# First stage with more landing places and a quarter-wise first B projection, and the modulation columns added at an earlier point of each group

## What is computed

```python
def modulation(cvec, w, b):                       # ada_w: 2048 x 12288
    return split(silu(cvec) @ w + b, 6, axis=-1)  # for c and for c_ctx

mx, mc = modulation(c, ada_w, ada_b), modulation(c_ctx, ada_w, ada_b)
hx = modulate(rms_norm(x, norm_g[0]), mx[0], mx[1])      # shift, scale
hc = modulate(rms_norm(ctx, norm_g[0]), mc[0], mc[1])
# mixer: z, x, B, C, dt = split(h @ w_in)  (w_in: 2048 x 10368), depthwise convolution of
# 3 taps and silu on x, B, C; dt = softplus(dt + bias); the scan over chunks, both directions;
# y * silu(z), norm, @ w_out
x = x + mx[2] * yx
h = modulate(rms_norm(x, norm_g[1]), mx[3], mx[4])
x = x + mx[5] * hier_moe(h)        # top-1 of 4 groups, top-2 of 8 experts
```

## Time and profile before

| | us |
|---|---|
| median of 3 runs (2378.75 to 2379.55) | 2378.75 |
| the profiled execution, its own time | 2375.91 |
| its span in the trace | 2374.4 |
| until the first product of the B projection | 152.3 |
| until the first product of the first x projection | 178.0 |
| one group in the hardware loop | 119.7 |
| expert loop, from its first weights in use | 1418.3 |

### The profile page before, as it was taken

One profiled execution on the slowest core, in us unless ns is written; L12 is line 12 of the kernel. 1 busy time (PEld: TensorE's weight loads), 2 busy tenths in 40 slices (PEclk: granted clock), 3 DMA queues, 4 the chain that ended last, 5 costly groups with the idle time before them and its releaser, 6 DMA issues. The chain is left out here.

```text
span 2374.4 us, 28701 instructions
## 1 busy us (share of the span) xinstructions
PE 2048.1 (86%) x10596; PEld 1224.0 (52%) x10596; DVE 1014.8 (43%) x1625; ACT 487.0 (21%) x513; POOL 108.4 (5%) x148
## 2 busy tenths in 40 slices
PE   4679989898989898986699669888888888888887
PEld 2248767676767777774588453333333333333332
DVE  2254555555656464644554552222222222222223
ACT  3133333333333333332344310000000000000000
POOL 0000000000000000000650000000000000000000
PEclk8689999999999999998899769999999999999999
DMA  6977556565656565654555519999999999999997
GB/s 220 323 228 242 174 175 182 178 181 176 181 176 181 175 182 175 186 174 163 181 195 195 195 58 404 422 422 422 422 422 422 422 422 422 422 422 422 422 422 318
DMA packets 296347, 660.37 MB, mean 278 GB/s; under 512 B 15936, under 2 KB 186304, under 8 KB 241904
## 3 DMA queue, kind: packets, MB, share of 16 engines
q1 hardware_dynamic: 288672, 635.27, 72.2%
q0 software_dynamic: 6672, 24.29, 2.7%
q10 hardware_dynamic: 960, 0.23, 0.0%
HBM read 653.28 MB, written 6.46 MB: 278 GB/s over the span
## 5 line engine op out<-in xcount | busy, mean ns | idle before, releaser
L1590 PE MATMUL bank<-wt,xe 128*64 128x512 f32 x2048 | 466.1, 597 | 110.8 <-DMA wt<-in_moe_w_up 107.4
L1371 PE MATMUL bank<-hTh,whi 128*128 128x256 f32 (+1 forms) x1280 | 417.2, 346 | 0.0
L1372 PE MATMUL bank<-hTl,whi 128*128 128x256 f32 (+1 forms) x1280 | 408.2, 339 | 0.0
L1263 DVE TENSOR_TENSOR x<-x,bank 128x512 f32<-128x512 f32 x256 | 158.5, 682 | 543.4 <-PE bank L1577 543.4
L1590 PEld LDWEIGHTS bank<-wt,xe 128*64 128x64 f32 x2048 | 158.2, 137 | 412.9 <-issue 409.2
L1371 PEld LDWEIGHTS bank<-hTh,whi 128*128 128x128 f32 x1280 | 246.1, 192 | 86.4 <-issue 62.0
L1372 PEld LDWEIGHTS bank<-hTl,whi 128*128 128x128 f32 x1280 | 246.1, 192 | 24.1
L866 DVE TENSOR_TENSOR wlo<-raw,whi 128x2048 fp32r<-128x2048 f32 x81 | 185.5, 2291 | 138.7 <-ACT whi L642 135.0
L1376 PE MATMUL bank<-hTh,wlo 128*128 128x256 f32 (+1 forms) x1280 | 234.9, 336 | 0.0
L1615 PE MATMUL bank<-wt,hdn 128*64 128x512 f32 x1024 | 226.8, 595 | 1.4 <-DVE hdn L1275 1.4
L1376 PEld LDWEIGHTS bank<-hTh,wlo 128*128 128x128 f32 x1280 | 199.8, 190 | 24.9
(11 more groups left out here) (281 smaller groups left out, 1821.9 us busy)
## 6 DMA issues: line engine op xcount, KB each, us to landing
wt<-in_moe_w_gate SPq DMA_DIRECT2D x128, 1024.0 KB, 23.4
wt<-in_moe_w_up SPq DMA_DIRECT2D x128, 1024.0 KB, 25.5
wt<-in_moe_w_down SPq DMA_DIRECT2D x128, 1024.0 KB, 22.4
raw<-in_ada_w SPq DMA_DIRECT2D x96, 1024.0 KB, 5.2
raw<-in_ssm_w_in SPq DMA_DIRECT2D x81, 1024.0 KB, 6.1
raw<-in_ssm_w_out SPq DMA_DIRECT2D x32, 1024.0 KB, 4.8
bc<-cum_d POOLq DMA_DIRECT2D x32, 512.0 KB, 7.0
y_d<-ybuf POOLq DMA_DIRECT2D x32, 128.0 KB, 4.5
```

Of the source, the lines that this page charges most:

```text
L1263: dve.tensor_tensor(x1[:, tt, cols], x1[:, tt, cols], banks[(1, 3, 6, 7)[nb]][:, :], ALU.add).then_inc(s_acc2, 1)
L1371: pe.matmul(bank[:, 0:width], wh[:, k, :], hTh[:, k, 0:width], start=(k == 0), stop=False)
L1372: last = pe.matmul(bank[:, 0:width], wh[:, k, :], hTl[:, k, 0:width], start=False, stop=False)
L1590: last = pe.matmul(banks[0][SLOTS * h:SLOTS * h + SLOTS, :], xe[:, k, :], wt[2 * q + h][:, FF * i:FF * i + FF], start=(k == 0), stop=(k == ...
```

## The change

It has two parts.

**First stage.** Six more places of 8 KB a partition (`fr0` to `fr5`) are laid over halves of tensors that are not yet written or no longer read: the upper halves of `hTh` and `hTl` and the second half of `xrows`. A table `FSLOT` gives each of the 33 positions one of nine places. The rows of `x` and `ctx` are issued ahead of all tiles. Blocks 0 and 1 both come before the transposes; blocks 2 to 5 follow, then half of the dt projection with half of the B projection (`b_part`), then blocks 6 and 7 and the other halves. The tile of the B weights is fetched right after the dt tile. ACT and DVE share the row scaling and the copies of `xnT`. The last three small parameter loads get a semaphore of their own, so TensorE's first transposes don't wait for them. The first B convolution stands inside the dt chain, and `dt_turn` with its copies comes after the first x projection, in other banks.

**Groups.** In step 5, DVE adds the modulation columns ahead of `store` and `weights(s, 1)`.

```diff
-    PRE = ADA1 + 1
+    FRONT = ADA1 + 1
+    FSLOT = [0, 1, 2, 3, 4, 5, 6] * 2 + [7, 8, 3, 4, 5, 6, 7, 8, 3, 4, 5, 6, 7, 8, 4, 6, 7, 8, 4]
+    PRE = RAW * FSLOT.count(0)
+        fr = [at(f"fr{i}", kb, [P, D]) for i, kb in enumerate((16, 24, 48, 56, 136, 144))]
...
@@ SyncE
-            for pos in range(PRE):
-                if pos == RAW:
-                    sp.dma_start(xrows[:, 0:2, :], ...x...).then_inc(s_x, 16)
-                    sp.dma_start(xrows[:, 2:4, :], ...ctx...).then_inc(s_x, 16)
-                if pos >= RAW:
-                    front_free(pos - RAW)
+            sp.dma_start(xrows[:, 0:2, :], ...x...).then_inc(s_x[0], 16)
+            sp.dma_start(xrows[:, 2:4, :], ...ctx...).then_inc(s_x[1], 16)
+            for pos in range(FRONT):
+                before = [q for q in range(pos) if FSLOT[q] == FSLOT[pos]]
+                if before:
+                    front_free(before[-1])
+                elif FSLOT[pos] >= 7:
+                    sp.wait_ge(s_xt, KC)
                 front_load(pos)
+                if pos == DT_POS:
+                    front_free(max(q for q in range(FRONT) if FSLOT[q] == 0))
+                    sp.dma_start(w_view(raw, 0), w_in[:, :, bass.ds(w_in_at(0, 0), P)]).then_inc(s_raw[0], 16)
...
@@ ScalarE
-            for tt in range(4):
+            for tt in (0, 2):
                 act.activation(xrows[:, tt, :], xrows[:, tt, :], ACT.Copy, scale=rstd[:, tt:tt + 1]).then_inc(s_xn, 1)
+            for k in range(1, KC, 2):
+                act.wait_ge(s_xt, k + 1)
+                act.activation(xnT[:, k, :], banks[k % 2][:, :], ACT.Copy).then_inc(s_xteA, 1)
...
             round_rows(0)
-            act.wait_ge(s_raw[DT_POS % RAW], 16 * (DT_POS // RAW + 1))
-            act.activation(whi[:, 0, :], raw[:, DT_POS % RAW, :], ACT.Copy).then_inc(s_hi, 1)
-            for j in range(1, len(BLOCK_PAIRS)):
+            round_rows(1)
+            act.wait_ge(front_sem(DT_POS), 16 * (FNTH[DT_POS] + 1))
+            act.activation(whi[:, 0, :], front_tile(DT_POS), ACT.Copy).then_inc(s_hi, 1)
+            conv_hi(0, 0)
+            for j in range(2, len(BLOCK_PAIRS)):
                 round_rows(j)
-            conv_hi(0, 0)
             conv_hi(0, 1)
...
+            conv_first(0, 0)
             act.wait_ge(s_du, 1)
             act.activation(dtw[:, 3, :], dtw[:, 2, :], ACT.Ln).then_inc(s_dln, 1)
...
@@ VectorE
             ada_rows(0)
-            for k in range(KC):
+            ada_rows(1)
+            for k in range(0, KC, 2):
                 dve.wait_ge(s_xt, k + 1)
-                dve.tensor_copy(xnT[:, k, :], banks[k % 2][:, :]).then_inc(s_xte, 1)
-            ada_rows(1)
+                dve.tensor_copy(xnT[:, k, :], banks[k % 2][:, :]).then_inc(s_xteV, 1)
             modulated(0)
...
             ada_rows(2)
             ada_rows(3)
-            lo(0, 0, raw[:, DT_POS % RAW, :], free=False)
             modulated(1)
+            lo(0, 0, front_tile(DT_POS), free=False)
+            conv_lo(0, 0)
...
             dve.tensor_scalar(dtw[:, U, :], dtw[:, E, :], 1.0, None, ALU.add).then_inc(s_du, 1)
+            drain(0, 0)
             dve.wait_ge(s_du, 1)
...
@@ VectorE, steps(g, w, ssd)
                     if w and n + 1 == NCH and not (isinstance(g, int) and g == GROUPS - 1):
                         conv_lo(g + 1, 0)
+                    if w and n == 5:
+                        ada_columns(g, 0)
...
                     if w and n == 8:
                         masked(g)
-                    if w and n == 5:
-                        ada_columns(g, 0)
-                    if w:
+                    if w and not (isinstance(g, int) and g == 0 and n == 0):
                         drain(g, n)
+                    if isinstance(g, int) and g == 0 and n == 2:
+                        dt_columns()
...
@@ TensorE
-            ada_block(0)
-            ada_turn(0)
+            for n in range(2):
+                ada_block(n)
+                ada_turn(n)
+            pe.wait_ge(s_xn, 4)
             for k in range(KC):
...
-            ada_block(1)
-            ada_turn(1)
-            for j in range(1, len(BLOCK_PAIRS)):
-                for n in (2 * j, 2 * j + 1):
-                    ada_block(n)
-                    ada_turn(n)
-                dt_part(j - 1)
-            dt_part(len(BLOCK_PAIRS) - 1)
+            for n in range(2, 6):
+                ada_block(n)
+                ada_turn(n)
+            for j in range(2):
+                dt_part(j)
+                b_part(j)
+            for n in range(6, 8):
+                ada_block(n)
+                ada_turn(n)
+            for j in range(2, 4):
+                dt_part(j)
+                b_part(j)
```

More of the change, by code:

```diff
@@ L74, in build @@
     assert L == 256 and LC == 256 and R == 8 and GC == 4 and ADA2 == NADA * GROUPS and TT == 2
-    PRE = ADA1 + 1
+    FRONT = ADA1 + 1
+    FSLOT = [0, 1, 2, 3, 4, 5, 6] * 2 + [7, 8, 3, 4, 5, 6, 7, 8, 3, 4, 5, 6, 7, 8, 4, 6, 7, 8, 4]
+    FNTH = [FSLOT[:pos].count(FSLOT[pos]) for pos in range(len(FSLOT))]
+    PRE = RAW * FSLOT.count(0)
+    assert len(FSLOT) == FRONT and FSLOT.count(0) == FSLOT.count(1) == FSLOT.count(2)
     BLOCK_PAIRS = [(j, NB1 // 2 + j) for j in range(NB1 // 2)]
@@ L79, in build @@
     DT_POS = 4 * NB1 // 2
-    SMALL = 12
+    SMALL = 9
     assert PRE % RAW == 0 and len(LOADS) % RAW == 0
@@ L245, in build @@
         s_pack = sem("s_pack")
-        s_x = sem("s_x")
+        s_small = sem("s_small")
+        s_x = [sem(f"s_xin{i}") for i in range(2)]
+        s_fr = [sem(f"s_fr{i}") for i in range(6)]
         s_const = sem("s_const")
@@ L372, in w_view, with front_tile, front_sem @@
             return ring[:, slot, :].rearrange("p (k n) -> p k n", k=KC)
+        def front_tile(pos):
+            j = FSLOT[pos]
+            return raw[:, j, :] if j < RAW else fr[j - RAW][:, :]
+        def front_sem(pos):
+            j = FSLOT[pos]
+            return s_raw[j] if j < RAW else s_fr[j - RAW]
         def raw_of(pos):
@@ L420, in slot_free @@
                 else:
-                    front_free(PRE - RAW + pos)
+                    front_free(max(q for q in range(FRONT) if FSLOT[q] == pos))
                     return
@@ L430, in group_loads @@
                 for pos, (kind, n) in enumerate(LOADS):
+                    if first and pos == 0:
+                        continue
                     slot_free(g, pos, first)
@@ L705, in steps @@
                     if w and n in CONV_AT:
[L706 to L714 removed]
+                        if not (isinstance(g, int) and g == 0 and n == 0):
+                            conv_first(g, n)
                     if ssd and n == 0:
@@ L1439, in c_times_b @@
                 pe.wait_ge(s_prod, NCH * g + 2)
-                if not (isinstance(g, int) and g == 0):
+                if isinstance(g, int) and g == 0:
+                    pe.wait_ge(s_tokm, 1)
+                else:
                     pe.wait_ge(s_stev, g)
```

151 lines of the change are left out of this document (81 added, 70 removed).

## The result

| | before | after |
|---|---|---|
| median, us | 2378.75 (2376.82 to 2379.55, 4 runs) | 2312.64 (2309.9 to 2315.62, 4 runs) |
| profiled execution, own time, us | 2375.91 | 2311.86 |
| its span, us | 2374.4 | 2310.3 |

The ratio is 0.9724 (95% interval 0.9711 to 0.9736). The forecast was 2312 us.

The account below looks back on a forecast made before the run. Bound taken: ahead of the expert loop, TensorE waits for DVE's addition in the groups and late tiles in the first stage. 52.8 + 13.7 + 0.3 = 66.8 us off 2378.75 gives about 2312 us, range 2303 to 2334.

Parts of the forecast that it names:

- Part 1: Groups 1 to 7, modulation tile: wait 1.85 instead of 7.73 us, clock kept; 7 x 7.54 = 52.8 us saved.
- the clock's: Tile and projection behind each group's wait: clock stays at 2.4 GHz, 6.82 instead of 8.48 us, 1.66 us saved.
- Part 2: First stage: transfers no longer idle for 20 us, dt projection ends at 138.6 instead of 152.28 us, 13.7 us saved.
- part 3: End of dt to first x projection: 24.5 instead of 25.7 us, less 0.9 us for `dt_turn`; net 0.3 us saved.
- 1.7 us for a slow start: First stage, each long run of dt and B products: 1.7 us added to 2.8 us per 12 products at full clock.
- In this time all places fill: First stage, during the 48 products: all landing places fill, so position 29 is issued only at about 109.7 us.
- The first: Groups: the clock falls (11.6 us less gain) or a new wait comes (7 to 14 us less); about 2324 us, chance 0.09.
- the wait at `y_chunk`: Groups: the 1.0 us margin is absent and a wait of 1 to 2 us a group comes, 7 to 14 us less gain.
- The second: First stage gains nothing: long runs of products at 1.2 GHz while the queue runs dry; about 2328 us, chance 0.12.
- third: Groups: the modulation tile is released by its tile or ACT's copy, not the addition; 2365 us, chance 0.02.
- The fourth: Groups: without waits the granted clock sinks below 1, making the kernel slower; about 2406 us at 0.90, chance 0.02.

Follow-up runs that it names:

- The pair of runs above: The changed kernel, 2312.64 us, and the same with ACT rounding the first x projection's weights ahead of the dt chain's last exponential: 2308.24 us, ratio 0.9699.
- columns alone: The kernel before with only the moved addition of the modulation columns in step 5: 2329.78 us, ratio 0.979.
- the stage alone: The changed kernel with the addition of the columns put back behind `masked`, so only the new first stage: 2361.22 us, ratio 0.9925.
- B behind dt: The changed kernel with all four first B projection quarters behind the dt projection, its first convolution and `drain` behind the logarithm and sums: 2302.76 us, ratio 0.968.
- x weights rounded early: Kernel of 2289.12 us (B behind dt, columns before chunk 6's subtraction, dt quarters 0, 1 at blocks 4, 5) plus x-weight rounding before the exponential: 2287.95 us.

## Why the prediction was right

**Part 1** was forecast at 52.8 us. The traces give 48.6 us: the first and the last of the seven tiles behind the waits start 1047.35 - 330.00 = 717.35 us apart before and 980.33 - 305.69 = 674.64 after, which is 42.7 for six groups, and the seventh wait gives its 5.9 and nothing behind it, since the clock fell there. The 1.85 us of idleness and the wait's releaser came exactly as read from the earlier trace rows. The term that was mis-sized is the clock's: 1.66 us x 7 was counted in full, and the clock fell behind 2 of the 7 waits, 2 x (8.28 - 6.82) = 2.9 us. The step that failed is "I take the clock as still at 2.4 GHz, since the fall came only 4.3 us into the longer wait": one long wait tells when the clock fell that time, not how early it can fall, and nothing of the products behind it, where it fell here (last section). The Trainium skill, page "TensorE: Matmul & The Clock Gate", section "HAM oscillation — how this bites in real kernels", stood against this term. Its example loses the clock in waits longer than these; here it was lost behind 10 of 42, so neither always nor never. The other 1.3 us are the price itself. It was read from group 2 alone, and against a like stretch of another step (6.82 us). From the tile's start to the first product of `y_chunk` the same work took these times, in before (groups 1 and 6) and in after:

```profile
330.00:338.65 8.65, 8.65 (x57) 6.81 (x57) 4.06 (x4) 0.63 (x1) 0.00 (x0) 0.78 0.58 164
928.20:936.46 8.26, 8.26 (x56) 6.42 (x56) 4.06 (x4) 0.63 (x1) 0.00 (x0) 0.82 0.60 167
```

```profile
305.69:312.60 6.91, 6.91 (x57) 5.91 (x57) 6.76 (x6) 0.91 (x1) 0.00 (x0) 1.00 0.85 261
```

The mean over the seven in before is 8.40, so a kept clock is worth 1.5 us and not 1.66.

**Part 2** was forecast at 13.7 us with 0.3 for part 3, and gave 18.4. The order of events was right to the step: DMA busy from 33 to 53 us, the stop near the end of the 48 products, idle time behind C. Nearly each size was a little too careful. The last quarter of block 5 was in use at 89.4 us (91.0 forecast), since the tiles went at 388 GB/s and not 367. From there to the end of the turn it took 3.2 us, not 4.9, at a higher clock. The 48 products took 11.2 us, not 12.9: their first one takes 0.47 us, so the clock was up from the start, and my 1.7 us for a slow start were not due. The row that the price had been checked against, 24 products in 7.32 us, has no slow start either: its first product takes 0.48 us, and the clock is down within the run, from 146 to 149.6 us; that the sum came out was luck. "In this time all places fill" was wrong as well, as said above; that `fr3` holds position 25 and stops the queue was right, and the stop lasted some 8 us, not 5. Together that makes 5.1 us earlier at the end of block 7's turn; the last 36 products then took 0.5 us longer than forecast.

**Part 3.** From the end of dt to the x projection it took 23.8 us (24.5 forecast). I had seen that TensorE would stand idle for 10 us or more, and took the chain as what sets it. The pair of runs above shows that it was one rounding's place. That doesn't change the number, but it was the larger thing to see. Behind it 1.8 us were lost again: the x projection started at 1.2 GHz after 11.95 us of idleness (13.2 us against some 12 before), and `dt_turn` came behind it.

**The sum** is right to 1 us by luck, because the misses cancel: 4.2 us too much in part 1, 4.4 too little in parts 2 and 3. At the start of the expert loop after is 1418.28 - 1352.18 = 66.1 us ahead, in the span 64.1. From the loop's first product to the end it is 956.1 us in before and 958.1 in after, but 956.9 to 957.8 in the twelve experiments, with the old first stage (columns alone, 957.3) as with the new (956.9 for the stage alone). So at most about 1 us of the 2 can be the change's; the rest is the spread of single executions, and what makes it is open.

**Rivals.** The first came in part (the clock, 3 us of its 11.6; the wait at `y_chunk` not). The second and third fell. The fourth fell too: the groups have mean clocks in the highest tenth.

## What to carry to other kernels

A wait's releaser is only the last of its conditions: before an edit takes it away, look up when each of the others was met, and expect the difference, not the wait. Where an in-order engine releases TensorE late, ask for each instruction ahead of the releasing one whether it must stand there; here one addition of 0.16 us was worth 49 us and one rounding 6. Work put in front of a chain "to fill a gap" costs most of its length if there is idle time behind the chain (here 6.3 us for three quarters of B that take 8.2), and in a stage fed through a few places a long run of it stops the transfers as well. When transfers stop, count the places that the next tile may go to, not the places that exist: here four of nine were in use, and two stood empty.

## What was not expected of the hardware

- The granted clock fell behind 10 of 42 waits of 1.85 us, behind none of 35 of 0.8 us and behind all of 5.5 and 7.7 us. The same instructions, group after group, ran behind it at 1.00 or at 0.79. What decides it in a given group is open. In none of the 10 had the clock fallen by the end of the wait: the granted clock in the wait is 1.00, the tile behind it still ran at 2.4 GHz (1.04 us; 1.89 us in before), and the first slow product started 1.0 to 1.6 us after the wait was over, with TensorE busy. In after, behind the wait that ends at 642.42 us, it was this one (0.28 us at 2.4 GHz):

```profile
643.77 0.41 PE L1429 MATMUL bank<-hTh,whi 128*128 128x256 f32 x1
```

- The same shows ahead of the first x projection: behind a wait of 3.5 us (B behind dt) its products began at 2.4 GHz and fell to 1.2 GHz some 1 us later; behind the shorter wait of 2.8 us (x weights rounded early) they began at 1.2 GHz, 0.77 us for the first.
- A run of 512-column products behind a turn and its wait of 1.09 us began at 2.4 GHz (0.47 us for the first, 0.23 from one to the next) at 92.5 us, and at 1.2 GHz (0.77 us) at 123.3 us: the same run behind the same short wait. The stretches ahead, in the windows of after, differ in TensorE's busy time, 8.09 of 10.50 us against 9.81 of 14.96:

```profile
82.00:92.50 10.50, 8.09 (x48) 3.35 (x48) 0.69 (x1) 0.00 (x0) 0.00 (x0) 0.75 1.04 387
108.30:123.26 14.96, 9.81 (x48) 3.48 (x49) 0.69 (x1) 0.00 (x0) 0.00 (x0) 0.60 1.07 368
```

- Tiles of 1 MB went at 385 to 388 GB/s with nine places, against 367 with three in what I had taken for full flow.
